# Scores in alternating row halves, later transposes of the probabilities, and a short convolution in PSUM

## What is computed

```python
def second_block(x, norm1_g, w_in, q_norm_g, k_norm_g, rel_bias, conv_w, pool_w,
                 pool_scale, w_out, norm2_g, w_mlp1, w_mlp2):
    h = rms_norm(x, norm1_g[l])
    p = jnp.einsum('bsd,de->bse', h, w_in[l])
    ...
    q = rms_norm(q, q_norm_g[l])
    k = rms_norm(k, k_norm_g[l])
    y_attn = chunked_band_attention(q, k, v, rel_bias[l])   # 8 heads of 64
    y_conv = gated_short_conv(gb, gc, hin, conv_w[l])
    y_pool = multiscale_pool(u, pool_w[l], pool_scale[l])
    mix = jnp.concatenate([y_attn, y_conv, y_pool], axis=-1)
    x = x + jnp.einsum('bse,ed->bsd', mix, w_out[l])
    h2 = rms_norm(x, norm2_g[l])
    f = jnp.square(jax.nn.relu(jnp.einsum('bsd,df->bsf', h2, w_mlp1[l])))
    x = x + jnp.einsum('bsf,fd->bsd', f, w_mlp2[l])

def gated_short_conv(gb, gc, hin, conv_w):
    z = gc * hin
    zp = jnp.pad(z, ((0, 0), (CONV_K - 1, 0), (0, 0)))
    y = sum(conv_w[i] * zp[:, i:i + s] for i in range(CONV_K))   # CONV_K = 3
    return gb * y
```

## Time and profile before

| | us |
|---|---|
| median of 3 runs | 732.14 |
| the runs | 732.50, 725.23, 732.14 |
| profiled execution, its own time | 733.28 |
| its span in the trace | 731.4 |
| TensorE busy | 716.5 (98%) |
| VectorE busy | 492.2 (67%) |
| GpSimd busy | 390.5 (53%) |
| ScalarE busy | 358.3 (49%) |

### The profile page before, as it was taken

The page is one execution under the profiler, slowest core; times in us unless marked ns, Lnnn a source line. Parts: engine busy times, 40 slices in busy tenths (PEclk is TensorE's granted clock), DMA queues, the critical chain, the costliest instruction groups (busy, mean ns, idle before and its releaser), DMA issues.

```text
span 731.4 us, 14173 instructions
## 1 busy us (share of the span) xinstructions
PE 716.5 (98%) x5848; PEld 694.0 (95%) x5848; DVE 492.2 (67%) x906; ACT 358.3 (49%) x459; POOL 390.5 (53%) x219
## 2 busy tenths in 40 slices
PE   6899999999999989999999999999999999999998
PEld 3798889999999989999999999999999999999998
DVE  3886897669536369877777775467946766666663
ACT  6688135245435456555555457435664434334331
POOL 0778553556548958878887887766877000000000
PEclk9999999999999989999999999999999999999999
DMA  8994888337534637555544555334344655655611
GB/s 358 419 413 167 345 310 312 127 116 257 210 115 169 205 112 293 177 192 202 184 173 175 187 205 184 120 122 163 125 165 161 216 204 176 225 182 174 221 58 58
DMA packets 21233, 145.84 MB, mean 199 GB/s; under 512 B 2481, under 2 KB 3249, under 8 KB 3890
## 3 DMA queue, kind: packets, MB, share of 16 engines
q1 hardware_dynamic: 21024, 144.87, 54.6%
q10 hardware_dynamic: 146, 0.07, 0.0%
HBM read 143.88 MB, written 1.05 MB: 198 GB/s over the span
## 4 chain that ended last, share of the span: by engine, by line
PE 94%; DVE 3%; issue 1%; ACT 1%; DMA 0%; DVEq 0%; ACTq 0%
PE bank L1445 24%; PE bank L1447 24%; PE bank L1446 24%; PE bank L1464 5%; PE CP L1446 2%; PE CP L1447 2%; PE CP L1445 2%; PE bank L1556 2%; PE bank L1489 1%; DVE ada_s L919 1%; DVE SPARE L919 1%; PE bank L1504 1%; PE CP L1478 1%; PE bank L1818 1%; PE bank L1471 0%
## 5 line engine op out<-in xcount | busy, mean ns | idle before, releaser
L472 POOL TENSOR_TENSOR wlo<-raw,whi 128x512 fp32r<-128x512 f32 (+1 forms) x185 | 354.7, 1947 | 144.4 <-ACT whi L490 143.6
L490 ACT ACTIVATE whi<-raw 128x2048 fp32r<-128x2048 f32 x100 | 191.0, 1911 | 54.8 <-DMA raw<-in_w_in 28.4
L1212 DVE SCALAR_TENSOR_TENSOR Y<-bank,vec,Y 128x189 f32<-128x189 f32 (+2 forms) x352 | 122.9, 421 | 41.3 <-ACT Y L745 41.3
L1445 PE MATMUL bank<-H2h,whi 128*128 128x256 f32 x352 | 100.4, 285 | 1.7 <-DVE H2l L1187 1.7
L1446 PE MATMUL bank<-H2l,whi 128*128 128x256 f32 x352 | 100.1, 284 | 0.0
L1447 PE MATMUL bank<-H2h,wlo 128*128 128x256 f32 x352 | 100.1, 284 | 0.0
L1445 PE MATMUL bank<-H1h,whi 128*128 128x256 f32 (+1 forms) x288 | 89.8, 312 | 2.7 <-DVE H1l L938 1.9
L1447 PE MATMUL bank<-H1h,wlo 128*128 128x256 f32 (+1 forms) x288 | 88.1, 306 | 0.0
L1446 PE MATMUL bank<-H1l,whi 128*128 128x256 f32 (+1 forms) x288 | 88.0, 306 | 0.0
L871 DVE TENSOR_TENSOR wlo<-raw,whi 128x2048 fp32r<-128x2048 f32 x29 | 66.4, 2292 | 31.6 <-ACT whi L490 31.6
L1445 PE MATMUL bank<-H4h,whi 128*128 128x256 f32 x256 | 70.9, 277 | 0.0
(11 more groups left out here) (329 smaller groups left out, 1920.7 us busy)
## 6 DMA issues: line engine op xcount, KB each, us to landing
raw<-in_w_mlp SPq DMA_DIRECT2D x32, 1024.0 KB, 4.9
raw<-in_w_in SPq DMA_DIRECT2D x30, 1024.0 KB, 6.1
raw<-in_ffn_up SPq DMA_DIRECT2D x22, 1024.0 KB, 4.9
raw<-in_ada_hi SPq DMA_DIRECT2D x16, 1024.0 KB, 5.2
raw<-in_ffn_down SPq DMA_DIRECT2D x11, 1024.0 KB, 4.8
raw<-in_w_out SPq DMA_DIRECT2D x8, 1024.0 KB, 4.8
ada_s<-in_ada_s SPq DMA_DIRECT2D x4, 1024.0 KB, 18.0
ada_p<-in_ada_p SPq DMA_DIRECT2D x2, 1024.0 KB, 10.2
```

The source lines that it names most:

```text
L472: m = e.tensor_tensor(l[:, a:a + step], r[:, a:a + step], h[:, a:a + step].bitcast(F32), ALU.subtract)
L490: e.activation(whi[q % NHI][:, :], raw[n % NRAW][:, :], ACT.Copy).then_inc(s["w_hi"], 1)
L1212: e.scalar_tensor_tensor(o[:, r0:r1, c0:c1], z[:, r0 + dr:r1 + dr, c0 + dc:c1 + dc], cw[:, f, tap:tap + 1], o[:, r0:r1, c0:c1], ALU.mult, ...
L1445: e.matmul(out, h[:, col:col + P], xh, start=first, stop=False, skip_group_check=True)
```

## The change

Four things are changed, all in the second block.

- Scores. `HORDER` now puts two even and two odd heads in each group. A group's scores go to three banks: `odd` and `even` for t = 1, `both` for t = 0 of all four heads. TensorE's order alternates between even heads (rows 0 to 63) and odd heads (rows 64 to 127), and it waits for its own `score_mm` count before an odd head writes to `both`. VectorE waits for the whole group before its first instruction and takes t = 1 first (`PARTS`).
- Transposes. `turn_probabilities(0)` stands after chunk 8 and `turn_probabilities(1)` after chunk 9. The products with the values of the first half wait only for the first three copies. ScalarE's order follows.
- Short convolution. `RR2` is `RR` squared; chunk 5 is multiplied by it, chunk 6 is multiplied by chunk 5 in its own bank (that is `Z`), chunk 7 by `RR` in its own bank, later by `YC`. VectorE's convolution is placed ahead of the last projection and the second probabilities. The banks of chunks 6 and 7 are freed by `conv_2` 7 and `mix_lo` 2.
- `w_out_2` takes the pool's k first, then the convolution's, then attention's.

```diff
-HORDER = [0, 2, 4, 6, 1, 3, 5, 7]
+HORDER = [0, 2, 1, 3, 4, 6, 5, 7]
+PARTS = [(1, 2, 2), (1, 0, 2), (0, 0, 4)]
...
-            e = [("proj", i + 1)] if i < 8 else [("val_2", 2 * i - 14)]
+            e = [("proj", i + 1)] if i < 6 else [("conv_2", 7)] if i == 6 else [("mix_lo", 2)] if i == 7 else [("val_2", 2 * i - 14)]
...
-MISC2 += [(f"sc{n}", "score", (4, 6, 8, 12, 14, 16)[n]) for n in range(6)]
+MISC2 += [(f"sc{n}", "score", (2, 4, 8, 10, 12, 16)[n]) for n in range(6)]
...
@@ vector: project_in @@
-            e.tensor_tensor(PP[:, at_:at_ + 2, :], two(product("w_in_2", i)[:, :]),
-                            RR[:, :].unsqueeze(1).to_broadcast([P, 2, T]), ALU.mult).then_inc(s["proj"], 1)
+            src = two(product("w_in_2", i)[:, :])
+            out = src if i >= 6 else PP[:, at_:at_ + 2, :]
+            if i == 5:
+                e.wait_ge(s["conv_2"], 1)
+            if i == 6:
+                e.wait_ge(s["proj"], 6)
+                by = PP[:, 14:16, :]
+            else:
+                by = (RR2 if i == 5 else RR)[:, :].unsqueeze(1).to_broadcast([P, 2, T])
+            e.tensor_tensor(out, src, by, ALU.mult).then_inc(s["proj"], 1)
@@ vector: scores @@
-            for m, (t, n0, per) in enumerate(((0, 4 * g, 4), (1, 4 * g, 2), (1, 4 * g + 2, 2))):
+            e.wait_ge(s["score_mm"], 3 * g + 3)
+            for m, (t, n0, per) in enumerate(PARTS):
+                n0 += 4 * g
                 ns = P * (t + 1)
                 b = bank[misc_bank[f"sc{3 * g + m}"]]
-                e.wait_ge(s["score_mm"], 3 * g + m + 1)
@@ vector: order @@
+        e.tensor_tensor(RR2[:, :], RR[:, :], RR[:, :], ALU.mult).then_inc(s["conv_2"], 1)
...
         probabilities(0)
+        short_conv()
         project_in(7)
         probabilities(1)
-        short_conv()
         e.wait_ge(s["conv_2"], 7)
         e.wait_ge(s["proj"], 8)
-        e.tensor_tensor(YC[:, :, :], YC[:, :, :], PP[:, 18:20, :], ALU.mult).then_inc(s["conv_2"], 1)
+        b = two(product("w_in_2", 7)[:, :])
+        e.tensor_tensor(b, b, YC[:, :, :], ALU.mult).then_inc(s["conv_2"], 1)
+        mix_low(b, 4, 2)
         for tp in range(2):
-            mix_low(two(bank[misc_bank[f"av{tp}"]][:, :]), 2 * tp, 2 + tp)
-        mix_low(YC[:, :, :], 4, 4)
+            mix_low(two(bank[misc_bank[f"av{tp}"]][:, :]), 2 * tp, 3 + tp)
@@ tensor: scores @@
+            odd, even, both = [misc(f"sc{3 * g + m}") for m in range(3)]
+            score(both, 0, g, 0, 0)
+            score(odd, 0, g, 2, 1)
+            score(both, P, g, 1, 0).then_inc(s["score_mm"], 1)
+            score(odd, T, g, 3, 1)
+            score(even, 0, g, 0, 1)
+            e.wait_ge(s["score_mm"], 3 * g + 1)
+            score(both, 2 * P, g, 2, 0)
+            score(even, T, g, 1, 1).then_inc(s["score_mm"], 1)
+            score(both, 3 * P, g, 3, 0).then_inc(s["score_mm"], 1)
@@ tensor: order @@
-            if i == 7:
-                turn_probabilities(0)
         for i in (8, 9):
             h, l = weights("w_in_2", i)
             by_tokens(group("w_in_2", i), h, l, H3h, H3l)
-            if i == 8:
-                turn_probabilities(1)
-        e.wait_ge(s["pt_done"], 6)
+            turn_probabilities(i - 8)
         for tp in range(2):
+            e.wait_ge(s["pt_done"], 3 * tp + 3)
...
-        order2 = [6, 7, 0, 1, 2, 3, 4, 5]
+        order2 = [6, 7, 4, 5, 0, 1, 2, 3]
```

More of the change, by code:

```diff
@@ L136 @@
          ("pool", "pool_out", 2), ("qkc3", "qk_rms", 4), ("kn0", "k_norm", 1), ("kn1", "k_norm", 2)]
-MISC2 += [(f"sc{n}", "score", (4, 6, 8, 12, 14, 16)[n]) for n in range(6)]
+MISC2 += [(f"sc{n}", "score", (2, 4, 8, 10, 12, 16)[n]) for n in range(6)]
 MISC2 += [(f"pt{n}", "pt_done", n + 1) for n in range(6)]
-MISC2 += [(f"av{n}", "mix_lo", n + 2) for n in range(2)] + [("col3", "rms_x", 2), ("rows3", "rr_done", 3)]
+MISC2 += [(f"av{n}", "mix_lo", n + 3) for n in range(2)] + [("col3", "rms_x", 2), ("rows3", "rr_done", 3)]
 def misc_tables():
@@ L218, in build @@
     RR1 = keep("RR1", [P, T])
+    RR2 = keep("RR2", [P, T])
     GG = keep("GG", [P, KT])
@@ L318, in build @@
     MXl = area("MXl", [P, KT, T], 48, F32R)
-    Z = area("Z", [P, 2, T], 20)
     YC = area("YC", [P, 2, T], 22)
@@ L823, in values_2 @@
                     "p (f c) -> p f c", f=2), ACT.Identity, scale=RC[:, 2 + t:3 + t]).then_inc(s["val_2"], 1)
+        values_2(8)
+        high(turn["w_in_2", 9] + 2)
         turn_probabilities(0)
-        high(turn["w_in_2", 9] + 2)
-        values_2(8)
+        e.wait_ge(s["conv_2"], 8)
+        e.activation(MXh[:, 4:6, :], two(product("w_in_2", 7)[:, :]), ACT.Copy).then_inc(s["mix_hi"], 1)
+        values_2(9)
         turn_probabilities(1)
-        values_2(9)
         for tp in range(2):
@@ L833, in scalar @@
                          ACT.Copy).then_inc(s["mix_hi"], 1)
-        e.wait_ge(s["conv_2"], 8)
-        e.activation(MXh[:, 4:6, :], YC[:, :, :], ACT.Copy).then_inc(s["mix_hi"], 1)
         warm(ACT.Sqrt)
@@ L1329, in short_conv @@
         def short_conv():
+            z = two(product("w_in_2", 6)[:, :])
             e.wait_ge(s["proj"], 7)
             e.wait_ge(s["qk_col"], 4)
-            e.tensor_tensor(Z[:, :, :], PP[:, 14:16, :], PP[:, 16:18, :], ALU.mult).then_inc(s["conv_2"], 1)
-            e.wait_ge(s["conv_2"], 1)
             for f in range(2):
-                e.tensor_scalar(YC[:, f, :], Z[:, f, :], cw2[:, f, 2:3], None, ALU.mult).then_inc(s["conv_2"], 1)
+                e.tensor_scalar(YC[:, f, :], z[:, f, :], cw2[:, f, 2:3], None, ALU.mult).then_inc(s["conv_2"], 1)
             for m in (1, 2):
@@ L1338, in short_conv @@
                 for f in range(2):
-                    e.scalar_tensor_tensor(YC[:, f, m:T], Z[:, f, 0:T - m], cw2[:, f, 2 - m:3 - m], YC[:, f, m:T],
+                    e.scalar_tensor_tensor(YC[:, f, m:T], z[:, f, 0:T - m], cw2[:, f, 2 - m:3 - m], YC[:, f, m:T],
                                            ALU.mult, ALU.add).then_inc(s["conv_2"], 1)
@@ L1809, in k_rows, with score @@
             m.then_inc(s["k_row"], 1)
-        def scores(g):
[L1812 to L1820, removed]
+        def score(b, col, g, n, t):
+            h = HORDER[4 * g + n]
+            lo_p, tile, ns = 64 * (h % 2), h // 2, P * (t + 1)
+            return e.matmul(b[:, col:col + ns], PP[lo_p:lo_p + 64, tile, t * P:(t + 1) * P],
+                            PP[lo_p:lo_p + 64, 4 + tile, 0:ns], start=True, stop=True)
+        def scores(g):
+            odd, even, both = [misc(f"sc{3 * g + m}") for m in range(3)]
[8 more added lines that the diff above has]
+            score(both, 3 * P, g, 3, 0).then_inc(s["score_mm"], 1)
         def turn_probabilities(g):
@@ L1877, in mixed @@
         def mixed(k):
-            n = {3: 1, 0: 2, 1: 3, 2: 4}[k // 2]
+            n = {3: 1, 2: 2, 0: 3, 1: 4}[k // 2]
             if k % 2 == 0:
```

## The result

The changed kernel takes 735.57 us at the median of 22 executions (727.74 to 736.17), the kernel before 732.45 (724.72 to 733.02), beside it on the same chip. The ratio is 1.0049, 95% interval 1.0027 to 1.0072: the change costs 3.1 us. (In all ratios here, executions over 1.5% above the fastest of the same kernel are left out; the lists of times have all of them.) I had forecast 729.9 us, and 723.5 to 733.0 as the range.

A forecast was written before the change was run, and what follows sets the result against it. TensorE, computing 716.5 of 731.4 us, was taken to bound the kernel. Scores −2.4 us plus 0.2 for chunk 9 gave −2.2, so 729.9 us as a median against 732.14; range 723.5 to 733.0 us.

The forecast's parts named there:

- the convolution's paragraph: Convolution from PSUM, bank releases and `w_out_2` order: nothing gained at the end itself; earlier gain kept to the end.
- point (5): Profile sign: `w_out_2` starts at about 526.5 us, and from there to the end stays 202.3 us.
- the two signs of being wrong: Wrong if the gain at `w_out_2` is not 1.7 to 2.6 us, or is there and gone by the end.
- Scores: Score products on TensorE: row halves overlap by a factor near 1.9, 1.62 us a group, saving 2.4 us in all.
- Rival B: Score products in different row halves run one after another, staying at 2.8 us; 732.1 to 732.5 us; chance 0.10.
- The added wait: TensorE's wait before odd heads write to the shared score bank: priced at nothing, upper bound 0.2 us a group.
- VectorE and the low half of chunk 9: VectorE's scores start later, GpSimd's low half ends at 516.1 to 516.6 us; TensorE waits 0.2 us, bounds 0 and 0.5.
- rival D: GpSimd's low half of chunk 9 ends at 518.9 us, TensorE waits 2.8 us; 732.5 us total; chance 0.08.
- Convolution: Six VectorE instructions from PSUM banks take 2.5 us, near 0.4 us each; worth nothing at the end.
- rival C: Bank of chunk 6 released late: convolution still 8.3 us, TensorE waits 4.6 us, 734.3 us total; chance 0.05.
- The gain at `w_out_2`: Start of `w_out_2` on TensorE comes 2.2 us earlier, with 1.7 to 2.6 us allowed.
- Noise: About 1% indistinguishable from no change; earlier runs spread over 7 us, one at 725.23; "same" got most of the chance.

The follow-up runs named there:

- e6: Kernel before with the four float32 row-product records issued once more ahead of chunk 2 of `w_mlp1`; 739.3 to 740.3 us, ratio 1.0117.
- e13: Changed kernel with the four float32 row-product records added ahead of chunk 1 of `w_out_2`; median 730.26 us.
- e2: Kernel before with the row `RR2` allocated but unused, shifting later areas by 1 KB; 731.43 us, ratio 0.9967.
- e3: Kernel before with only the score products alternating between the row halves; 732.79 us, ratio 0.9988.
- e8: Kernel before with only the transposes of the probabilities moved a chunk later; median 733.05 us, ratio 1.0005.
- e4: Kernel before with only the convolution in PSUM, its place, freed banks and the order of `w_out_2`; 732.01 us, ratio 1.0004.
- e14: Kernel before with the four float32 row-product records added ahead of chunk 1 of `w_out_2`; 732.30 us.
- e16: Kernel before with the four float32 row-product records added ahead of chunk 2 of `w_out_2`; ten executions at 731.7 to 733.5 us.
- e1: Changed kernel with the four float32 row-product records in `w_mlp1` issued twice, ahead of its second chunk; median 729.54 us.
- e7: Changed kernel without the overwritten row products ahead of chunk 1 of `ffn_up`; 721.1, 721.5, 727.7 and 734.7 us.
- e5: Changed kernel with the four float32 row-product records issued once more ahead of chunk 2 of `w_mlp1`; median 732.81 us.

## Why the prediction was wrong

The step that failed is the last of the convolution's paragraph: that the next low half "follows TensorE, so the gain is kept to the end", and with it point (5), "the distance from there to the end is as before, 202.3 us". It is 29.63 + 178.67 = 208.3 us, the second of the two signs of being wrong that its last sentence names. There is no more waiting there than before. I had looked for a loss only in waits, and taken a product's length to be the same whatever comes before. The runs showed that it has two values, that it is set where TensorE's stream is broken, and that it then holds until the stream is broken again: 117.7 ns where the last stage had 113.3, times 1491, is the 6.5 us.

The steps ahead of it:

- **Scores.** Right, and better than taken. The two groups stand at 490.39 to 491.90 and 494.16 to 495.67 us, 1.51 us each where I had 1.62 and before had 2.82. A whole group is thus faster by a factor of 1.87. With the estimate of 0.25 us for the change of shape, which no run isolates, it is 1.26 of 2.57 us of streaming, a factor of 2. Records of both halves stand at the same time:

```profile
490.39 0.37 PE L1825 MATMUL CP<-PP 64*128 64x128 f32 x1
490.40 0.48 PE L1825 MATMUL bank<-PP 64*128 64x256 f32 x1
490.61 0.38 PE L1825 MATMUL CP<-PP 64*128 64x128 f32 x2
490.72 0.38 PE L1825 MATMUL bank<-PP 64*128 64x256 f32 x1
...
491.90 0.38 PE L1456 MATMUL bank<-H3h,whi 128*128 128x256 f32 x1
```

  Rival B falls. The Trainium skill ("TensorE: Matmul & The Clock Gate", Part 3, measured speedup) gives a factor for four row tiles only; the 1.54 that I had estimated from it is below the 1.87 that this trace shows for whole groups. The added wait costs nothing.
- **VectorE and the low half of chunk 9.** Right. VectorE's first score is 492.12 − 490.39 = 1.73 us behind the first product (forecast 1.82), the low half starts 502.20 − 490.39 = 11.81 us behind it (before 11.34, forecast + 0.5). Chunk 9 of `w_in_2` begins 18.14 us behind it, where I had 18.1 to 18.6 (516.1 to 516.6 less 498.03), after a wait of 0.38 us (I had 0.2, with 0.5 as the bound). Its low half is what it waited for: the four parts end at 508.42, in 6.2 us (I had 6.7), and rival D falls. The bank of chunk 6 had been free since 507.38:

```profile
492.12 1.66 DVE L1301 SCALAR_TENSOR_TENSOR SCR<-bank,RC,BI 128x256 f32<-128x256 f32 x4 [4.47 <-PE CP L1825]
502.20 6.22 POOL L473 TENSOR_TENSOR wlo<-raw,whi 128x512 fp32r<-128x512 f32 x4 [7.30 <-ACT whi L491]
508.53 0.35 PE L1475 MATMUL bank<-whi,H3h 128*128 128x256 f32 x1 [0.38 <-issue]
```

- **Convolution.** Right. Its six instructions take 2.7 us (504.70 to 507.38; forecast 2.5, before 8.3); rival C falls:

```profile
504.70 0.86 DVE L1344 TENSOR_SCALAR YC<-bank,vec 128x256 f32<-128x256 f32 x2
505.60 1.78 DVE L1348 SCALAR_TENSOR_TENSOR YC<-bank,vec,YC 128x255 f32<-128x255 f32 x4
```

- **The gain at `w_out_2`.** −2.57 us where I had −2.2 and allowed 1.7 to 2.6. It is −2.61 for the scores and +0.38 for the wait; the remaining −0.34 us is −0.66 in the products of the chunks, of which the short pitch gives 114 × 4.5 ns = 0.51, and +0.32 in the transposes and the products with the values. The sum had none of these, so that the last 0.3 us of the agreement is luck. The short pitch also gives the −0.89 us in `w_out_2`, which the changed kernel runs at 276 ns: 64 × 3 products by 4.5 ns are 0.86.
- **Noise.** I had read the run at 725.23 us as spread. It was one stage, 7 us, and "same" had 0.9 of the chance because I took a difference of that size to be nothing that a profile could show.

What is shown: that the last stage's pitch makes the 6.5 us (e6, e13), that addresses don't (e2), and that a break put into `w_out_2` brings the changed kernel's last stage back (e13). What is only seen in the profiles: that scores or transposes alone are enough to bring `w_out_2` to the short pitch (e3, e8) and the convolution alone is not (e4), so the way in from the products with the values seems to set it. Open is what inside the engine makes the two pitches, and whether chunk 0 of `w_mlp1` comes out at either pitch because `w_out_2` ends short or because TensorE then waits in the column sums.

## What to carry to other kernels

Where an engine is busy without a gap, compare the length of its commonest instruction stage by stage, at the median, before looking for waits: here 276 against 281 ns was worth twice the whole change. When times of one kernel fall into groups some fixed amount apart, find the stage that makes the step, and judge a change within a group; a change of 3 us ahead of a long unbroken stream can give it back by how it enters that stream. Where the order allows it, look at what stands at the entry of a long stream (here four small products) as something to be tried with and without.

## What the runs showed of the hardware

- Two pitches of the same product (128 rows, 128 columns of weights, 256 streamed, float32r): 113.3 and 117.7 ns at the same granted clock of 1.00. Once entered, a pitch held for 1491 products in before and after. At the long pitch one weight load of three lasts 192 ns and not 188, always that of the same product within a stream.
- Four float32 records of 128 columns between two such streams set it anew. Over the 18 profiles, where TensorE did not wait at the break, a short pitch turned to the long one 18 times of 18. A long one turned to the short one 13 times and stayed 3 times (once each in e8, e14 and e16), and in these three the long load was that of the high-by-high product. With about 0.04 us of idle time inside the break a long pitch turned twice (e3, and e1 with its eight records) and stayed once (e8). With a wait of about 0.1 us, a short pitch went to the long one in after and e7 and stayed short in e5.
- Two 64-row groups of float32 products in different halves of the rows and different banks run at the same time: 1.51 us a group where 2.82 stood, 1.26 of 2.57 us of streaming by the estimate of 0.25 us for the change of shape.
